# A two-block transformer kernel: column-group sums for the convolution norms, and the norms' learned scale and shift on another engine

## The chip, the cores and the metric

The kernel runs on one core of one Trainium2 chip. The metric is the device time of one execution in microseconds. One run of the program computes both blocks of the reference for one sequence of 256 tokens, all in 32-bit floats.

## The reference

The first block has two layers on 256 tokens of width 1024. Each layer projects the tokens, runs a gated depthwise convolution of 31 taps over 512 channels with a layer norm and a SiLU behind it, runs a neighbourhood attention of 8 heads, and mixes both. The first layer has a dense feed-forward part, the second a mixture of 8 experts of which each token takes 2. Each layer also adds a gated embedding product. The second block has two layers of window attention and mLSTM, and isn't touched here.

```
def first_block(...):
    h = layer_norm(x, ln_in_g, ln_in_b)
    for i in range(DEPTH):
        ...
        conv_out = conformer_conv(a, g, conv_w[i], conv_b[i], conv_ln_g[i], conv_ln_b[i])
        attn_out = neighbourhood_attention(qkv[:, :, 0], qkv[:, :, 1], qkv[:, :, 2], rpb[i])
        mix = jnp.concatenate([conv_out, attn_out], axis=-1) @ w_out[i] + b_out[i]
        h = layer_norm(DEEPNORM_ALPHA * h + mix, ln1_g[i], ln1_b[i])
        j = i // 2
        if i % 2 == 0:
            f = swiglu(h, ffn_w1[j], ffn_w3[j], ffn_w2[j])
        else:
            f = moe_swiglu(h, w_router[j], moe_w1[j], moe_w3[j], moe_w2[j])
        e = jax.nn.sigmoid(h @ ple_gate_w[i] + ple_gate_b[i]) * (p[i] @ ple_w[i])
        h = layer_norm(DEEPNORM_ALPHA * h + f + e, ln2_g[i], ln2_b[i])
    return h
```

## The kernel before, in words

Features lie on the 128 partitions and tokens along the free axis, so the 1024 features are 8 chunks of 128x256 (`KC` = 8) and the 512 convolution channels are 4 (`CC` = 4). The program is written out by hand, one instruction stream for each engine: TensorE (PE), VectorE (DVE), ScalarE (ACT) and the queue of SyncE (SP), which issues all loads. The streams meet at semaphores. The order of the work is the order in which it is written; no scheduler moves it. `fill` names a PSUM bank and waits until the bank's last reader is done; `tile` is the reader's wait for that bank.

**Weights** come as units of 1 MB. SP loads them ahead in a ring of 6 slots, and of 13 in the expert stage (`ring_places`). `load` waits until PE has used the slot's last unit. The addresses of the expert units depend on the routing, so SP waits for `order_out` (L2348, the cast that ends `by_tokens`) before it issues the first of them, and from there on SP runs as far ahead as the slots let it.

[...] `norm_mean` multiplies every chunk by a 128x128 matrix of ones, one full matrix product for each chunk. Where a norm is in `FOLDED_MEAN` or `FOLDED_VAR`, the sum is made otherwise: `group_sum` gives each of four chunks its own group of 32 columns (`COL`), the four products lie side by side, ACT copies the parts to SBUF (`parts_copy`, L1651), and one more product of 128x256 adds them up (`fold_parts`). The norms `conv0` and `conv1` are made in the plain way before. For them PE makes the mean after the first of two value units in `block1_projection` (L592), and the variance at its end. ACT makes the inverse root (L1630), DVE scales (L2155), ACT applies the SiLU with the learned scale and shift (`conv_silu`, L1719), and in `half_pair` PE waits for all four chunks (`conv_mixed`). Ahead of that, `condition_turns` waits for `cond_row`, an ACT copy (L1663) that stands behind `conv_silu` in ACT's stream.

**The learned scale and shift** of the norms `in`, `ln1_0`, `ln2_0`, `ln1_1` and `ln2_1` are DVE instructions (`layer_gain`, L2172) that alternate with the scaling of the next chunk (L2155). Each raises `norm_out`, for which the matrix products of the next stage wait chunk by chunk.

**The routing** of layer 1 follows `ln1_1`. In `router_beside_embedding` PE computes the logits, a 128x8 product for each chunk and each 128 tokens, with one of the last four products of the embedding behind each of the first four chunks. It then transposes the tokens (`turn_tokens`, L800) and waits in `places` for `chosen_out`. DVE ranks the experts of each token in `routing`: five dependent instructions for each half of the tokens, then the choice (L2311), then a copy and four instructions for the gate weights (L2313 to L2318). `by_tokens` takes the counts from PSUM (L2334) and ends in `order_out`. PE goes on with a gate unit, `gather`, and the expert groups.

## Time and profile before

| | |
|---|---|
| Median of 3 runs | 1993.35 us (1993.34 to 1994.25) |
| The profiled execution | 1994.45 us |
| Its span in the trace | 1992.4 us |
| PE busy | 1965.0 us, 99% |
| DVE busy | 753.0 us, 38% |
| ACT busy | 404.5 us, 20% |
| Weights and inputs read | 507.40 MB, 255 GB/s over the span |

Times in the trace count from the span's start; the span is about 2 us shorter than the execution's own time, since what lies ahead of the first instruction and behind the last isn't in it. The stages are, roughly: first norm to 15.6 us, layer 0 to 399, of which the dense feed-forward part is 157 to 386, layer 1 up to the routing to 531, routing and gathering to 564, the experts to 1410, and the second block to the end. A 32-bit product appears in the trace as two records. The engine name PEld is TensorE's weight load.

### The profile page before, as it was taken

Reading aid. Unit: us, or ns where it says so; the run is one execution under the profiler, and the core shown is the slowest. Engines: PE = TensorE matmul, PEld = TensorE weight load, DVE = VectorE, ACT = ScalarE, POOL = GpSimd, SP = SyncE. Lnnn points to the kernel's source line nnn. Section 1 sums busy time; section 2 is a strip of 40 time slices with the busy share of each in tenths; the row PEclk is TensorE's granted clock in tenths of the full one; section 3 lists DMA queues with packets and bytes.
Section 4 is the critical chain, followed back from the end, with each engine's and each line's share of the span. In section 5 each row is a group of like instructions: output and inputs, shape, how many; then the busy total and the mean of one; then the engine's idle time right before and its main releaser. Section 6 shows DMA issues by size and latency. Waiting matters only on the chain.

```text
span 1992.4 us, 36529 instructions
## 1 busy us (share of the span) xinstructions
PE 1965.0 (99%) x15708; PEld 1422.1 (71%) x15708; DVE 753.0 (38%) x1766; ACT 404.5 (20%) x953; POOL 0.2 (0%) x4
## 2 busy tenths in 40 slices
PE   9999999999999999999999999999999999999998
PEld 8879999888766656666666666556664578566797
DVE  6847555586511111111111111111317734426725
ACT  1242110104310111000100010000214442223343
POOL 0000000000000000000000000000000000000000
PEclk9999999999999999999999999999999999999999
DMA  9473644544299999999999999999321211122220
GB/s 353 171 296 146 210 169 176 189 171 190 78 420 420 421 420 421 420 420 420 415 420 420 420 421 419 420 420 420 138 106 55 95 48 59 64 106 85 106 85 22
DMA packets 74929, 510.86 MB, mean 256 GB/s; under 512 B 7888, under 2 KB 13200, under 8 KB 13968
## 3 DMA queue, kind: packets, MB, share of 16 engines
q1 hardware_dynamic: 74768, 508.51, 63.7%
q8 instruction: 126, 2.06, 0.4%
q14 instruction: 35, 0.29, 0.0%
HBM read 507.40 MB, written 1.08 MB: 255 GB/s over the span
## 4 chain that ended last, share of the span: by engine, by line
PE 93%; DMA 4%; DVE 2%; ACT 1%; issue 0%; SPq 0%; DVEq 0%; ACTq 0%
PE ps L483 91%; DMA ring<-weights 4%; PE ps L1313 1%; PE ps L852 1%; PE ps L713 0%; DVE work L2155 0%; SPq L1581 0%; DVE xc L2172 0%; DVE spare L2776 0%; DVE work L2167 0%; PE ps L1473 0%; DVE small L2951 0%; ACT work L1964 0%; ACT work L1630 0%; DVE work L2948 0%
## 5 line engine op out<-in xcount | busy, mean ns | idle before, releaser
L483 PE MATMUL ps<-work 128*32 128x256 f32 (+8 forms) x4912 | 515.6, 375 | 3.2 <-DVE work L2471 0.9
L483 PE MATMUL ps<-work,ring 128*128 128x256 f32 (+2 forms) x1992 | 503.9, 407 | 1.0 <-DVE work L2916 1.0
L483 PEld LDWEIGHTS ps<-work 128*32 128x32 f32 (+3 forms) x4912 | 344.9, 142 | 134.0 <-issue 68.4
L483 PEld LDWEIGHTS ps<-work,ring 128*128 128x128 f32 x1992 | 338.9, 190 | 138.0 <-issue 110.6
L483 PE MATMUL ps<-ring,work 128*32 128x256 f32 (+3 forms) x4392 | 405.8, 407 | 2.7 <-DMA ring<-weights 2.1
L483 PEld LDWEIGHTS ps<-ring,work 128*32 128x32 f32 (+1 forms) x4392 | 234.3, 120 | 129.2 <-issue 59.3
L483 PE MATMUL ps<-xc,ring 128*128 128x256 f32 (+1 forms) x1344 | 254.9, 350 | 1.9 <-DVE xc L2172 1.9
L483 PEld LDWEIGHTS ps<-xc,ring 128*128 128x128 f32 x1344 | 223.5, 191 | 34.4 <-issue 7.3
L2429 DVE TENSOR_TENSOR work<-work,ps 128x256 f32<-128x256 f32 x42 | 17.7, 422 | 411.2 <-ACT work L1797 411.2
L1797 ACT ACTIVATE work<-ps 128x256 f32<-128x256 f32 x42 | 16.2, 385 | 556.1 <-PE ps L483 556.1
L483 PE MATMUL ps<-spare,work 128*32 128x256 f32 (+1 forms) x1128 | 120.4, 427 | 2.5 <-DMA ring<-weights 1.3
L483 PE MATMUL ps<-xc,work 128*128 128x256 f32 (+1 forms) x624 | 117.2, 346 | 0.0
L483 PEld LDWEIGHTS ps<-xc,work 128*128 128x128 f32 x624 | 102.7, 191 | 16.3 <-issue 4.2
L2204 DVE SCALAR_TENSOR_TENSOR work<-work,par 128x256 f32<-128x256 f32 x240 | 98.0, 480 | 0.9
L2392 DVE TENSOR_TENSOR work<-ps,work 128x512 f32<-128x512 f32 x68 | 47.1, 692 | 92.7 <-PE ps L483 92.4
L483 PEld LDWEIGHTS ps<-spare,work 128*32 128x32 f32 x1128 | 52.2, 110 | 38.3 <-issue 21.6
L2550 DVE TENSOR_TENSOR work<-ring 128x512 f32<-128x512 f32 x52 | 33.6, 688 | 51.1 <-PE ps L483 51.1
L483 PE MATMUL ps<-work,con 128*32 128x256 f32 (+1 forms) x262 | 45.3, 390 | 5.8 <-DVEq L2501 1.5
L2443 DVE TENSOR_TENSOR work<-work 128x512 f32<-128x512 f32 x14 | 9.7, 693 | 97.6 <-ACT work L1803 97.6
L483 PE MATMUL ps<-xc,spare 128*128 128x256 f32 x192 | 44.3, 392 | 0.0
L483 PEld LDWEIGHTS ps<-xc,spare 128*128 128x128 f32 x192 | 37.3, 196 | 7.8 <-issue 1.7
L483 PEld LDWEIGHTS ps<-work,con 128*32 128x32 f32 (+1 forms) x262 | 27.8, 151 | 19.0 <-issue 7.9
(284 smaller groups left out, 1254.8 us busy)
## 6 DMA issues: line engine op xcount, KB each, us to landing
ring<-weights SPq DMA_DIRECT2D x287, 1024.0 KB, 13.6
work<-weights SPq DMA_DIRECT2D x130, 1024.0 KB, 19.2
spare<-weights SPq DMA_DIRECT2D x54, 1024.0 KB, 18.9
work<-rel SPq DMA_DIRECT2D x8, 512.0 KB, 12.7
spare<-rows SPq DMA_DIRECT2D x2, 2048.0 KB, 9.2
con<-consts SPq DMA_DIRECT2D x1, 1368.0 KB, 22.1
work<-x_t SPq DMA_DIRECT2D x1, 1024.0 KB, 4.9
xc<-ctx_t SPq DMA_DIRECT2D x1, 1024.0 KB, 27.2
```

Of the source, the lines that this page charges most:

```text
L483: ins = eng.matmul(o, lhs, rhs, start=start, stop=stop, **kw)
L852: last = eng.transpose(o[:, k * P:k * P + P], pair_a[:, n % 2, k * P:k * P + P], ident)
L1313: last = eng.transpose(o[:, kt * P:kt * P + P], prob2_flat[:, at:at + P], ident)
L1797: eng.activation(pair_s[:, n % 2, :], o[:, 0:GW], ACT.Silu).then_inc(s["pair_silu"], 1)
L2204: ins = eng.scalar_tensor_tensor(out=conv_acc[:, j, :], in0=src, scalar=w, in1=conv_acc[:, j, :], op0=ALU.mult, op1=ALU.add)
L2392: return eng.tensor_tensor(r, o.rearrange("p (a b) -> p a b", b=T), r, ALU.add)
L2429: eng.tensor_tensor(pair_a[:, n % 2, :], pair_s[:, n % 2, :], o[:, GW:2 * GW], ALU.mult)\
L2443: eng.tensor_tensor(v, v, rows(gate_row, 2), ALU.mult).then_inc(s["first_weighted"], 1)
L2550: ins = eng.tensor_tensor(up_sum(i, z), in0, in1, op)
```

## The change

Four things are changed. The norms `conv0` and `conv1` are summed on column groups, with the fold of the mean in the middle of the second value unit and the fold of the variance behind the first condition rows of `block1_attention`. The learned scale and shift of `in`, `ln1_0`, `ln2_0` and `ln1_1` become ACT instructions (`gain`); DVE then only scales. The last four embedding products stand behind all logits. On DVE the routing comparisons of both token halves are one instruction each, and the gate weights are made after `by_tokens`. `mean_parts`, `var_parts` and `fold_parts` get a bank and a number of chunks, and `token_sums` waits for `norm_out`, which another engine raises now.

```diff
@@ -78,8 +78,8 @@
-FOLDED_MEAN = ["in", "ln2_0", "ln2_1"]
-FOLDED_VAR = ["ln1_0", "ln2_0", "ln1_1", "ln2_1", "rms0"]
+FOLDED_MEAN = ["in", "conv0", "ln2_0", "conv1", "ln2_1"]
+FOLDED_VAR = ["conv0", "ln1_0", "ln2_0", "conv1", "ln1_1", "ln2_1", "rms0"]
@@ -504,34 +504,35 @@
-            def group_sum(o, c, v):
+            def group_sum(o, c, v, chunks=KC):
 
                 q = COL * (c % 4)
-                return mm(o[q:q + COL, 0:T], ones[:, 0:COL], v, c < 4, c >= 4)
+                return mm(o[q:q + COL, 0:T], ones[:, 0:COL], v, c < 4, c >= chunks - 4)
...
@@ -614,10 +615,13 @@
                     w = next_unit()
                     o = fill(("v", l, j), 4 + j, (s["v_out"], 2 * l + j + 1))
                     tokens(w, GW, o[:, 0:T], xc, 0)
+                    if j:
+                        fold_parts("mean", f"conv{l}", 2)
                     tokens(w, GW, o[:, T:2 * T], xc, 1).then_inc(bank_full[4 + j], 1)
                     if j == 0:
-                        norm_mean(f"conv{l}", conv_acc, CC, T, 2)
-                norm_var(f"conv{l}", CC, T, True, 2)
+                        mean_parts(f"conv{l}", conv_acc, 2)
+                for _ in var_parts(f"conv{l}", True, 3):
+                    pass
@@ -662,6 +666,7 @@
             def block1_attention(l):
                 eng.wait_ge(s["cond_ready"], 1)
                 condition_rows(l, 0)
+                fold_parts("var", f"conv{l}", 2)
@@ -775,21 +780,20 @@
                     if c == KC - 1:
                         last.then_inc(bank_full[0], 1)
-                    if c < 4:
-                        next(products)
-                assert next(products, "ended") == "ended"
+                for _ in products:
+                    pass
...
-                o = fill(("counts",), 1, (s["order_out"], 1))
+                o = fill(("counts",), 6, (s["order_out"], 1))
...
-                o = fill(("places",), 0, (s["places_out"], 1))
+                o = fill(("places",), 4, (s["places_out"], 1))
@@ -1633,6 +1637,13 @@
+            def gain(name, g, b, first=0, end=KC):
+
+                for c in range(first, end):
+                    eng.wait_ge(s["norm_scaled"], before(name) + c + 1)
+                    eng.activation(xc[:, c, 0:T], cen[:, c, :], ACT.Identity, bias=par[:, PC(b, c)],
+                                   scale=par[:, PC(g, c)]).then_inc(s["norm_out"], 1)
+
@@ -2082,6 +2093,7 @@
             eng.wait_ge(s["params_loaded"], 16)
+            gain("in", "ln_in_g", "ln_in_b")
@@ -2092,7 +2104,10 @@
                 norm(f"ln1_{l}", KC, T)
-                ple_products(l)
+                gain(f"ln1_{l}", f"ln1_g{l}", f"ln1_b{l}", 0, 4)
+                ple_products(l, 0, 1)
+                gain(f"ln1_{l}", f"ln1_g{l}", f"ln1_b{l}", 4)
+                ple_products(l, 1)
@@ -2101,7 +2116,9 @@
                     norm("ln2_0", KC, T)
+                    gain("ln2_0", "ln2_g0", "ln2_b0", 0, 2)
                     condition_rows(1, -1)
+                    gain("ln2_0", "ln2_g0", "ln2_b0", 2)
@@ -2294,23 +2311,24 @@
+                eng.tensor_copy(by_expert[:, 4], con[:, CN.all("bases")])
...
-                for t in range(TT):
-                    other = logits[:, t, :].unsqueeze(1).broadcast_to([P, 8, 8])
...
-                    link(eng.tensor_tensor(gc, other, own, ALU.is_gt))
-                    link(eng.tensor_tensor(ge, other, own, ALU.is_equal))
-                    link(eng.tensor_tensor(ge, ge, before, ALU.mult))
-                    link(eng.tensor_tensor(gc, gc, ge, ALU.add))
-                    link(eng.tensor_reduce(rank_t[:, t, :], gc, AX.X, ALU.add))
+                other = logits.unsqueeze(2).broadcast_to([P, TT, 8, 8])
+                own = logits.unsqueeze(3).broadcast_to([P, TT, 8, 8])
...
+                eng.tensor_tensor(gc, other, own, ALU.is_gt)
+                link(eng.tensor_tensor(ge, other, own, ALU.is_equal))
+                link(eng.tensor_tensor(ge, ge, before.unsqueeze(1).broadcast_to([P, TT, 8, 8]), ALU.mult))
+                link(eng.tensor_tensor(gc, gc, ge, ALU.add))
+                link(eng.tensor_reduce(rank_t, gc, AX.X, ALU.add))
                 eng.tensor_scalar(rank_t, rank_t, float(TOP_K), None, ALU.is_lt).then_inc(s["chosen_out"], 1)
                 eng.wait_ge(s["chosen_out"], 1)
-                link(eng.tensor_copy(by_expert[:, 4], con[:, CN.all("bases")]))
+
+            def gate_weights():
+
                 eng.wait_ge(s["gate_exp"], 2)
@@ -3029,10 +3049,11 @@
-                norm(f"ln1_{l}", res, KC, T, layer_gain(f"ln1_g{l}", f"ln1_b{l}", xc))
+                norm(f"ln1_{l}", res, KC, T, None)
                 if l == 1:
                     routing()
                     by_tokens()
+                    gate_weights()
                     places()
@@ -3040,7 +3061,7 @@
-                norm(f"ln2_{l}", res, KC, T, layer_gain(f"ln2_g{l}", f"ln2_b{l}", xc))
+                norm(f"ln2_{l}", res, KC, T, layer_gain("ln2_g1", "ln2_b1", xc) if l else None)
```

PE's stream at the end of `block1_projection` and the start of `block1_attention`, before (`work,con` is a sum with the matrix of ones, `ring,work` with 32 rows the condition rows, 128x2x2 the condition turns, the last row the first `half_pair`):

```order
L483 MATMUL ps<-ring,xc 128x256 x16
L483 MATMUL ps<-work,con 128x256 x4
L483 MATMUL ps<-ring,xc 128x256 x16
L483 MATMUL ps<-work,con 128x256 x4
L483 MATMUL ps<-ring,work 32x256 x16
L483 MATMUL ps<-work 128x256 x4
L483 MATMUL ps<-ring,work 32x256 x16
L483 MATMUL ps<-con,work 128x2x2 x2
L483 MATMUL ps<-work,ring 128x256 x8
```

and with the change:

```order
L483 MATMUL ps<-ring,xc 128x256 x16
L483 MATMUL ps<-work,con 32x256 x4
L483 MATMUL ps<-ring,xc 128x256 x8
L483 MATMUL ps<-work,con 128x256
L483 MATMUL ps<-ring,xc 128x256 x8
L483 MATMUL ps<-work,con 32x256 x4
L483 MATMUL ps<-ring,work 32x256 x16
L483 MATMUL ps<-work,con 128x256
L483 MATMUL ps<-work 128x256 x4
L483 MATMUL ps<-ring,work 32x256 x16
L483 MATMUL ps<-con,work 128x2x2 x2
L483 MATMUL ps<-work,ring 128x256 x8
```

Each sum of four full products became four on column groups and one fold; the fold of the variance is 16 condition-row products later than the sum was.

PE's stream at the routing, before against after (`par,xc` are the logits, `work,ring` the embedding products, `con,xc` the transposes):

```order
-L483 MATMUL ps<-par,xc 128x8 x2
-L483 MATMUL ps<-work,ring 128x256
-L483 MATMUL ps<-par,xc 128x8 x2
-L483 MATMUL ps<-work,ring 128x256
-L483 MATMUL ps<-par,xc 128x8 x2
-L483 MATMUL ps<-work,ring 128x256
-L483 MATMUL ps<-par,xc 128x8 x2
-L483 MATMUL ps<-work,ring 128x256
-L483 MATMUL ps<-par,xc 128x8 x8
-L800 MATMUL ps<-con,xc 128x128 x16
+L483 MATMUL ps<-par,xc 128x8 x16
+L483 MATMUL ps<-work,ring 128x256 x4
+L804 MATMUL ps<-con,xc 128x128 x16
```

The 16 logit products now stand in one piece, and the four embedding products between them and the transposes.

ACT's stream at norm `ln2_0` with the change (L1634 is the inverse root, L1644 the gain, L1674 the copy of the condition row for which PE waits):

```order
L1634 ACTIVATE work<-ps,con 128x256
L1644 ACTIVATE xc<-work,par 128x256 x2
L1674 ACTIVATE work<-ps 128x256
L1644 ACTIVATE xc<-work,par 128x256 x6
L1719 ACT_TABLE_LOAD
```

Before, the copy stood directly behind the inverse root; now two gains are ahead of it.

## Rows read from the trace of the kernel before

**Rows 1.** Windows, experts: stretch, length, busy PE/PEld/DVE/ACT/POOL, clock, DMA share, GB/s
```profile
564.00:1410.00 846.00, 840.31 (x8986) 535.02 (x8987) 104.31 (x186) 74.09 (x162) 0.00 (x0) 1.00 1.01 419
```

**Rows 2.** Chain of waits, late in the expert stage: start us, us, what
```profile
1319.04 26.87 DMA ring<-weights
1346.04 3.66 PE ps L483 x64
```

**Rows 3.** Waits of the whole span, PE on weights: total us, times, longest
```profile
PE ps L483 <- DMA ring<-weights: 3.4, 4, 1.3
```

**Rows 4.** Timeline, PE and DVE, first norm: start us, us, engine, line [idle before]
```profile
15.64 14.70 PE L483 MATMUL ps<-xc,ring 128*128 128x256 f32 x61 [0.57 <-DVE xc L2172]
...
15.09 0.41 DVE L2172 TENSOR_SCALAR xc<-work,par 128x256 f32<-128x256 f32 x1
...
19.04 0.73 DVE L2172 TENSOR_SCALAR xc<-work,par 128x256 f32<-128x256 f32 x2
```

**Rows 5.** Groups of ACT by shape, modulate: busy us, mean ns
```profile
L1700 ACT ACTIVATE work<-work,small 128x256 f32<-128x256 f32 x16 | 8.1, 588 | 2.4 <-DVE work L2683 2.4
```

**Rows 6.** Timeline, PE, start of the dense feed-forward stage
```profile
154.61 2.02 PE L483 MATMUL ps<-xc,ring 128*128 128x128 f32 x16 [0.73 <-DVE xc L2172]
156.91 2.02 PE L483 MATMUL ps<-xc,ring 128*128 128x128 f32 x16 [0.28 <-DVE xc L2172]
```

**Rows 7.** Timeline, PE and ACT, norm ln2_0
```profile
397.45 0.61 PE L483 MATMUL ps<-con,work 128*128 128x4 f32 x4 [0.84 <-ACT work L1663]
398.39 6.89 PE L483 MATMUL ps<-xc,ring 128*128 128x256 f32 x22 [0.33 <-DVE xc L2172]
...
397.03 0.38 ACT L1663 ACTIVATE work<-ps 128x256 f32<-128x256 f32 x1
```

**Rows 8.** Timeline, PE, a sum on column groups and what follows it
```profile
527.60 0.64 PE L483 MATMUL ps<-work,con 128*32 128x256 f32 x8
528.17 1.13 PE L483 MATMUL ps<-work,ring 128*128 128x256 f32 x4
```

**Rows 9.** Timeline, PE, around the variance sum of conv0
```profile
80.90 7.07 PE L483 MATMUL ps<-ring,xc 128*128 128x256 f32 x32
87.81 1.89 PE L483 MATMUL ps<-work,con 128*128 128x256 f32 x8
89.63 1.93 PE L483 MATMUL ps<-ring,work 128*32 128x256 f32 x32
...
94.42 0.61 PE L483 MATMUL ps<-con,work 128*128 128x4 f32 x4
94.89 3.70 PE L483 MATMUL ps<-work,ring 128*128 128x256 f32 x16
```

**Rows 10.** Timeline, ACT, around the same sum
```profile
89.74 0.47 ACT L1630 ACTIVATE work<-ps,con 128x256 f32<-128x256 f32 x1 [6.76 <-PE ps L483]
...
93.51 0.36 ACT L1663 ACTIVATE work<-ps 128x256 f32<-128x256 f32 x1
```

**Rows 11.** Timeline, PE, logits and routing
```profile
535.10 1.85 PE L483 MATMUL ps<-par,xc 128*128 128x8 f32 x16
537.21 1.97 PE L800 MATMUL ps<-con,xc 128*128 128x128 f32 x16 [0.27 <-DVE small L2294]
540.39 1.25 PE L483 MATMUL ps<-small,con 128*128 128x8 f32 x10 [1.21 <-DVE small L2311]
541.50 8.84 PE L483 MATMUL ps<-xc,spare 128*128 128x256 f32 x32
```

**Rows 12.** Timeline, DVE, routing after the choice
```profile
541.31 0.17 DVE L2334 COPY work<-ps 128x8 f32<-128x8 f32 x1
...
543.45 0.17 DVE L2348 CAST crowded<-work 128x8 int32<-128x8 f32 x1
```

**Rows 13.** Windows around both falls of the clock, columns as in Rows 1
```profile
399.00:403.00 4.00, 4.00 (x12) 2.95 (x12) 3.75 (x14) 0.00 (x0) 0.00 (x0) 0.57 0.69 244
542.00:547.00 5.00, 5.00 (x17) 4.09 (x16) 4.62 (x19) 0.00 (x0) 0.00 (x0) 0.66 0.22 66
```

More of the change, by code:

```diff
@@ L505, in norm_mean @@
                 last.then_inc(bank_full[bank], 1)
-            def group_sum(o, c, v):
+            def group_sum(o, c, v, chunks=KC):
                 q = COL * (c % 4)
-                return mm(o[q:q + COL, 0:T], ones[:, 0:COL], v, c < 4, c >= 4)
-            def mean_parts(name, src):
-                o = fill(("mean_parts", name), 0, (s["norm_sums"], SUMS["mean", name]))
-                for c in range(KC):
+                return mm(o[q:q + COL, 0:T], ones[:, 0:COL], v, c < 4, c >= chunks - 4)
@@ L515, in mean_parts @@
+            def mean_parts(name, src, bank=0):
+                o = fill(("mean_parts", name), bank, (s["norm_sums"], SUMS["mean", name]))
+                for c in range(chunks_of(name)):
                     if normk(name) > 1:
                         eng.wait_ge(*source(name, c))
-                    last = group_sum(o, c, src[:, c, 0:T])
-                last.then_inc(bank_full[0], 1)
-            def var_parts(name, centred):
-                o = fill(("var_parts", name), 1, (s["norm_sums"], SUMS["var", name]))
-                for c in range(KC):
+                    last = group_sum(o, c, src[:, c, 0:T], chunks_of(name))
+                last.then_inc(bank_full[bank], 1)
@@ L524, in var_parts @@
+            def var_parts(name, centred, bank=1):
+                chunks = chunks_of(name)
+                o = fill(("var_parts", name), bank, (s["norm_sums"], SUMS["var", name]))
+                for c in range(chunks):
                     eng.wait_ge(s["norm_squared"], before(name) + c + 1)
-                    last = group_sum(o, c, squares(name, centred)[:, c, 0:T])
-                    if c == 3:
+                    last = group_sum(o, c, squares(name, centred)[:, c, 0:T], chunks)
+                    if c == chunks - 1:
+                        last.then_inc(bank_full[bank], 1)
+                    if c % 4 == 3:
@@ L527, in var_parts, with fold_parts @@
                         yield
-                last.then_inc(bank_full[1], 1)
-                yield
-            def fold_parts(kind, name):
-                b, read_by = (1, (s["norm_sums"], SUMS["std", name])) if kind == "var" else \
-                    (0, (s["norm_centered"], before(name) + KC))
+            def fold_parts(kind, name, bank=0):
+                b, read_by = (bank + 1, (s["norm_sums"], SUMS["std", name])) if kind == "var" else \
+                    (bank, (s["norm_centered"], before(name) + chunks_of(name)))
@@ L1750, in block1_attention, with ple_products @@
                             .then_inc(s["nbr_turned"], 1)
-            def ple_products(l):
-                for c in range(4):
+            def ple_products(l, first=0, end=KC // 2):
+                for c in range(first, end):
                     o = tile(eng, "ple", l, c)
@@ L3023, in _ @@
             eng.wait_ge(s["x_loaded"], 16)
-            norm("in", res, KC, T, layer_gain("ln_in_g", "ln_in_b", xc), beside=prepare)
+            norm("in", res, KC, T, None, beside=prepare)
             for l in range(DEPTH):
```

10 lines of the change are left out of this document (5 added, 5 removed).

## The prediction

> **What bounds the kernel now.** The first page shows PE busy for 99% of the span, so only PE's own work, its few waits and its clock can be worth anything; DVE and ACT idle most of the time. I then cut the span by stage. The expert stage holds 846 of the 1992 us, and in it two things are full at once: PE is busy for 840.31 us and the 16 DMA engines have a share of 1.01 at 419 GB/s [rows 1]. The chain of waits says which of the two ends last: late in the stage it runs through a weight transfer of 26.87 us, which PE waits for at 1346.04 us [rows 2]. PE waits only 3.4 us for weights in all, in four places [rows 3]. So the transfers, running without a pause from the first expert unit on, set the end of the stage, and PE is some 3.4 us ahead of them. That stage ends earlier by as much as its first load is issued earlier, which is the moment of `order_out`, and what PE alone gains behind the routing is lost in a longer wait for weights. Everything ahead of `order_out` counts in full if it lies on PE's path. Behind the experts nothing is changed.
>
> **First norm.** The first product of the projection starts at 15.64 us, just behind the first gain, and the eight gains of DVE run from 15.09 us to 19.04 + 0.73 = 19.77 us [rows 4], slower than the 0.43 us in which PE eats a chunk (two records of 7.07/32 = 0.22 us each, [rows 9]). On ACT the trace has the same kind of instruction, an activation with scale and shift from SBUF: 588 ns long, 8.1/16 = 0.51 us apart [rows 5]. It starts when DVE has scaled the first chunk, about 14.87 us, so the first chunk comes at 15.46 us where DVE's came at 15.50, and the last at 15.46 + 7 x 0.51 = 19.0 us. **Gain 0.8 us.**
>
> **`ln1_0`.** PE waits for chunk 3 until 154.61 us and for chunk 7 until 156.91 us [rows 6]. From the same first scaling (151.82 us) ACT delivers chunk 3 at 154.0 us, then makes one copy of embedding products (0.5 us), and delivers chunk 7 at 156.5 us. With 0.14 us from gain to PE the second wait ends at 156.6 us. **Gain 0.3 us.** DVE's token sums start earlier and bind nothing.
>
> **`ln2_0`.** Here the order on ACT costs something. PE's last condition turns wait for the row copy, which ends at 397.41 us [rows 7]. With the change two gains stand ahead of it, and the first can't start before 397.62 us, so the copy ends at 397.62 + 2 x 0.51 + 0.38 = 399.0 us and the projection starts at about 399.5 us where it started at 398.39 [rows 7]. The gains then come faster than before. The clock matters too: between 399 and 403 us the granted clock averages 0.57, that is, mostly 1.2 GHz, after PE had waited 0.84 and 0.33 us and had done small products between [rows 7, 13]. PE does its first products at half clock either way and enters that stretch later. I take **a loss of 0.8 us**; the bounds are 1.1 us lost (the whole delay) and 0.2 us gained (at full clock the last chunk ends the first product, and it comes 0.2 us earlier).
>
> **The convolution norms.** A sum of four full products takes 89.63 - 87.81 = 1.82 us [rows 9]; four on column groups take 528.17 - 527.60 = 0.57 us [rows 8], and the fold is one product more, 0.43 us. That is 0.8 us of PE for each of two sums in each of two layers, 3.3 us in all. But the fold of the variance comes behind the condition rows, and everything on ACT comes behind the fold. Before, ACT started the inverse root at 89.74 us and was done with root, table load, four SiLUs and the row copy at 93.51 + 0.36 = 93.87 us [rows 10], 4.13 us later, and PE wanted the row at 94.42 us [rows 9]: slack 0.55 us. Now relative to the start of the variance sum: rows start at +0.57, the fold at +2.4, the root at +3.1 (before: +1.93), so the row is copied at +7.2, while PE arrives at 6.61 - 1.82 + 0.57 + 0.43 = +5.8. PE waits 1.4 us and resumes 0.6 to 0.7 us later than before, against the 0.7 to 0.8 us that the mean's sum, which has no such wait behind it, saved. On the way the scores wait for the root too, since their bank is the one that it reads, but that wait is inside the same 1.4 us. **Net nothing in each layer**; the bounds are 1.5 us gained, where the chain is shorter than its rows, and 0.5 us lost.
>
> **Logits and routing.** Before, PE paced the logits: the last four chunks end at 535.10 + 1.85 = 536.95 us [rows 11]. Now the first chunk is there at 531.33 us, a chunk follows every 0.51 us (one copy between), and the last at 535.3 us, so the logits end at about 535.9 us, 1.05 us earlier. The embedding products (4 x 0.43 us) and the transposes (1.97 us, [rows 11]) follow without a wait, and PE reaches the counts at 539.4 us where it was at 540.39. It had waited 1.21 us there for DVE's choice [rows 11]; now DVE has five dependent instructions fewer (10 of 0.26 us became 5 of about 0.3) and is done at about 538.2 us, so PE comes last, and DVE's saving is worth only what it takes out of that wait. DVE took the counts at 541.31 us [rows 12], 0.4 us after they were there, because the gate weights came first; now it takes them at 539.95. The 2.3 us up to the cast [rows 12] are unchanged. At full clock `order_out` comes **1.35 us earlier**. The gate weights are paid behind it, where PE is busy with a gate unit of 8.84 us [rows 11] and hides them.
>
> **The clock in this place.** After the waits of 0.27 and 1.21 us, with 128x8 products around the second, the clock fell: 0.66 on average from 542 to 547 us [rows 13], and 32 records took 8.84 us [rows 11] that take 7.07 at 2.4 GHz [rows 9], a price of 1.77 us, free before, since the expert stage waits for weights anyway. In the dense stage idle times of 0.73 and 0.28 us with wide products between them did no such thing (the first there stayed 2.02 us long, [rows 6]). So narrow products seem to count almost as idle time, and the change puts all 16 of them in one piece of over 4 us. I expect the clock to fall during or behind it, in front of `order_out`, where the slower products and transposes are on the path. If it falls on those wholly the price is 1.77 us, if early part of it hides in the pace of ACT; I take 1.2 us, bounds 0 and 2.5. The Trainium skill (TensorE: Matmul & The Clock Gate, HAM oscillation) says that only long idle gaps of TensorE throttle it again; the trace disagrees, with falls after waits of 1.21 us at most. By the rule the clock would stay up here, which is the first rival.
>
> **The sum**, against the profiled execution's 1994.45 us: -0.8 - 0.3 + 0.8 + 0 - 1.35 + 1.2 = -0.45 us, so 1994.0. The median, 1993.35 us, is 1.1 us below that execution; I apply the difference to it: **1992.9 us**. No difference is to be measured: 0.2%, 4 us, is about what a measurement of this kernel can tell from no change.
>
> **Rivals.**
> A, the clock holds through the logits: 0.45 + 1.2 us off the median, so **1991.7 us**. For it: PE has almost no idle time there, only narrow products. Against it: the contrast above.
> B, the new wait in the convolution norms becomes the dearer side, and the kernel is **slower**. Two idle stretches of about 0.7 us each, with narrow turns beside them, are like those ahead of the fall at 399 us [rows 13]. If the clock falls behind them, the next products take 1.77 us more in that layer: 1992.9 + 1.8 = 1994.7 us with one layer, 1996.4 with both. It decides when PE's waits between fold and turns pass roughly the 1.2 us of [rows 7]. Against it: between the two stand 32 wide records of condition rows.
> C, the fold's chain is short and PE hardly waits: the two waits of 1.4 us fall away, about **1990.1 us**. It needs ACT to finish 1.4 us sooner than its rows say.
> D, the transfers don't bind the expert stage, and PE's start there counts: it gains 1.0 us for the counts and 1.77 us for a gate unit at full clock in place of the net 0.15 us, about **1990.3 us**. The saturated DMA and the chain speak against it [rows 1, 2].
>
> **How the numbers follow.** The forecast 0.52, A 0.2, B 0.13, C 0.06, D 0.04, the rest for something unseen. Between them they span 1990.1 to 1996.4 us. The range 1990.2 to 1995.4 leaves out C's lower side, B with both layers, and most of the unseen. None of the named cases passes 4 us: faster by over 0.2% 0.06 (C with A), slower by over 0.2% 0.04 (B in both layers with the worst bounds), 0.90 in between.
>
> **What would show it.** The first projection's opening wait unchanged, but its first unit about 0.8 us shorter; PE idle twice before the turns of each attention stage, the turns waiting for the row copy by over 0.5 us; turns of `ln2_0` 1.5 us later against the copy of the variance; a granted clock of 0.50 somewhere between 533 and 541 us and none on the gate unit; the cast of the routing within 0.5 us of its old place; PE's waits for weights in the expert stage growing from 3.4 us to 5 or more. It would be wrong if `order_out` moved by 1 us or more, if conv waits were absent, or if the expert stage got shorter than from `order_out` to its end before.

## The result, and the profile after

| | before | after |
|---|---|---|
| Median of 19 runs each | 1993.36 us (1992.27 to 1994.59) | 1998.12 us (1996.68 to 2000.16) |
| The profiled execution, its span | 1994.45, 1992.4 us | 1999.24, 1997.5 us |
| Cast of the routing (`order_out`) starts | 543.45 us | 548.18 us |
| From the cast to the last instructions of the chain | 1443.9 us | 1444.3 us |

The ratio of after to before is 1.0024, interval 1.0018 to 1.0030. The kernel is **slower by 4.8 us**, and the prediction was wrong: 1992.9 us, with a range up to 1995.4 us.

The last two lines of the table say where to look. The chain of waits of the changed kernel has these late pieces (start us, us, what), the first two of the same kind as those in [rows 2]:

```profile
1323.32 28.04 DMA ring<-weights
1351.50 3.66 PE ps L483 x64
...
1992.45 2.38 DVE work L2184 x6
```

The last wait for weights ends at 1351.50 us, where it ended at 1346.04 us: 5.5 us later. The last DVE instructions start at 1992.45 us; in the chain of before they start at 1987.34 us. From the start of the cast to the end of that weight wait it is 803.3 us, before 802.6 us. So the expert stage only shifted with the cast, as the prediction says of it, and all of the loss is made ahead of 548.18 us. The window of the expert stage answers to [rows 1] (stretch, length, busy PE, PEld, DVE, ACT, POOL, clock, DMA share, GB/s), and the waits of PE for weights to [rows 3] (total us, times, longest):

```profile
564.00:1410.00 846.00, 837.82 (x8965) 534.67 (x8967) 105.96 (x188) 73.68 (x163) 0.00 (x0) 1.00 1.01 420
```

```profile
PE ps L483 <- DMA ring<-weights: 4.4, 3, 2.2
```

PE waits 1.0 us more for the ring. Behind the routing it had gained 1.7 us (its first gate unit takes 7.15 us now, not the 8.84 of [rows 11]), and the stretch from the cast to the end is none the shorter. That the gain turned into just these waits isn't shown: x4_three below has the same 7.15 us and waits 3.6 us in all.

**First norm and `ln1_0`.** PE's timeline (start us, us, engine, line, operation, output<-input, tile, count, and in brackets the idle time before and what ended it), to be held against [rows 4, 6]:

```profile
14.90 2.36 PE L483 MATMUL ps<-xc,ring 128*128 128x256 f32 x9 [0.61 <-ACT xc L1644]
...
156.22 2.02 PE L483 MATMUL ps<-xc,ring 128*128 128x128 f32 x16 [0.42 <-ACT xc L1644]
```

The start at 14.90 us isn't the change's: the variance sum of the first norm already begins at 9.24 us where it began at 10.01. Over all traces of this case that start lies anywhere from 8.95 to 10.12 us, so I count every place below from it. From there to the mean sum of `conv0` (79.18 us before, 77.59 after) it is 69.17 us before and 68.35 us after: the gains on ACT are worth **0.82 us**.

**The convolution norm.** PE, DVE and ACT around both sums of `conv0`, columns as above. These rows answer to [rows 9, 10]:

```profile
77.59 0.64 PE L483 MATMUL ps<-work,con 128*32 128x256 f32 x8
...
81.71 0.59 PE L483 MATMUL ps<-work,con 128*128 128x256 f32 x2
...
85.69 0.64 PE L483 MATMUL ps<-work,con 128*32 128x256 f32 x8
87.26 1.93 PE L483 MATMUL ps<-ring,work 128*32 128x256 f32 x32 [0.93 <-issue]
89.13 0.70 PE L483 MATMUL ps<-work,con 128*128 128x256 f32 x2
90.48 1.13 PE L483 MATMUL ps<-work 64*128 64x256 f32 x8 [0.66 <-ACT work L1634]
91.55 1.93 PE L483 MATMUL ps<-ring,work 128*32 128x256 f32 x32
94.14 0.58 PE L483 MATMUL ps<-con,work 128*128 128x4 f32 x4 [0.66 <-ACT work L1674]
...
84.28 2.28 DVE L2250 TENSOR_TENSOR work<-work,con 128x2048 f32<-128x2048 f32 x1
86.48 0.68 DVE L2258 TENSOR_TENSOR work<-ps,par 128x512 f32<-128x512 f32 x1
...
89.86 0.47 ACT L1634 ACTIVATE work<-ps,con 128x256 f32<-128x256 f32 x1 [3.08 <-PE ps L483]
...
93.63 0.36 ACT L1674 ACTIVATE work<-ps 128x256 f32<-128x256 f32 x1
```

PE is idle three times: 0.93 us ahead of the first condition rows, 0.66 us for the inverse root (L1634) and 0.66 us for the copied row (L1674). The last two I had foreseen, as 1.4 us; the rows show 1.32. The first I had not. The condition rows go to bank 5, and the last reader of bank 5 is DVE's bias add to the second value unit (L2258), which ends at 86.48 + 0.68 = 87.16 us, behind the mask of 2.28 us. The profile gives this wait only as "issue"; that it is the bank, x5_bank shows below. Before, the full variance sum of 1.82 us [rows 9] stood in front of the same rows and covered this read. DVE in the trace of before:

```profile
83.04 2.28 DVE L2233 TENSOR_TENSOR work<-work,con 128x2048 f32<-128x2048 f32 x1
...
88.01 0.69 DVE L2241 TENSOR_TENSOR work<-ps,par 128x512 f32<-128x512 f32 x1 [2.69 <-PE ps L483]
```

There the mask was done at 85.32 us, DVE sat idle until PE had filled the bank, and the bias add began 0.20 us behind the start of the variance sum (87.81 us). In the changed kernel it begins 0.79 us behind it (85.69 us), because the mean comes later: it is folded in the middle of the second value unit, and DVE's subtraction of it and the mask come behind the fold. So by the rows about 0.6 of the 0.93 us comes from the mean's late fold, and only the rest from the shortened variance sum alone. This split is an estimate; no run folds the variance alone.

From the mean sum to the turns it is 94.14 - 77.59 = 16.55 us, before 94.42 - 79.18 = 15.24: **1.31 us lost**. Layer 1 shows the same three waits.

**`ln2_0`.** PE and ACT, answering to [rows 7]:

```profile
398.35 1.02 PE L483 MATMUL ps<-con,work 128*128 128x4 f32 x4 [2.42 <-ACT work L1674]
399.23 21.14 PE L483 MATMUL ps<-xc,ring 128*128 128x256 f32 x85
...
396.94 1.09 ACT L1644 ACTIVATE xc<-work,par 128x256 f32<-128x256 f32 x2 [0.49 <-DVE work L2172]
397.94 0.36 ACT L1674 ACTIVATE work<-ps 128x256 f32<-128x256 f32 x1
```

PE waits 2.42 us in one piece where it waited 0.84 us. Behind the start of this wait its clock is low, and for longer than before, which the windows below show.

**Logits and routing.** PE and DVE, answering to [rows 11, 12]:

```profile
534.33 2.00 PE L483 MATMUL ps<-par,xc 128*128 128x8 f32 x16 [0.46 <-ACT xc L1644]
536.69 2.94 PE L483 MATMUL ps<-par,xc 128*128 128x8 f32 x16 [0.36 <-ACT xc L1644]
539.48 3.76 PE L483 MATMUL ps<-work,ring 128*128 128x256 f32 x8
543.03 2.56 PE L804 MATMUL ps<-con,xc 128*128 128x128 f32 x16
...
546.46 7.15 PE L483 MATMUL ps<-xc,spare 128*128 128x256 f32 x32
...
541.74 0.17 DVE L2327 TENSOR_SCALAR small<-small 128x16 f32<-128x16 f32 x1
546.04 0.17 DVE L2352 COPY work<-ps 128x8 f32<-128x8 f32 x1 [4.13 <-PE ps L483]
...
548.18 0.17 DVE L2366 CAST crowded<-work 128x8 int32<-128x8 f32 x1
```

DVE has its choice at 541.9 us and then waits 4.13 us for PE. PE is late because it works at half clock. Eight records of embedding products take 3.76 us; at 2.4 GHz eight such records take 1.97 us (below, in the kernel with fillers). From the first logit to the cast it is 13.85 us, before 543.45 - 531.51 = 11.94 us. The windows around both falls of the clock, columns as in [rows 1]:

```profile
397.00:401.00 4.00, 2.65 (x8) 2.37 (x9) 2.56 (x10) 4.00 (x9) 0.00 (x0) 0.57 0.29 123
401.00:405.00 4.00, 4.00 (x12) 3.19 (x11) 0.00 (x0) 1.52 (x2) 0.00 (x0) 0.57 0.83 315
537.00:541.00 4.00, 4.00 (x19) 3.73 (x19) 1.24 (x7) 2.07 (x5) 0.00 (x0) 0.57 0.00 0
541.00:545.00 4.00, 4.00 (x19) 3.44 (x18) 0.81 (x4) 1.71 (x2) 0.00 (x0) 0.58 0.00 0
```

A mean of 0.57 over 4 us is 3.4 us at 1.2 GHz and the rest at 2.4. Each fall lasts 6.8 us here; each of those in [rows 13] lasted 3.4 us.

**The account up to the cast**, in us, counted from the variance sum of the first norm, after less before: first norm -0.82, `conv0` +1.31, `ln1_0` -0.41, `conv1` +1.31, `ln2_0` +2.2, routing 13.85 - 11.94 = +1.91. The sum is +5.5. The cast moved by 4.73, since this execution began its variance sum 0.77 us earlier. The figure for `ln2_0` is the stretch from its first condition turns to the first logit (141.23 us before, 144.74 after) without the 1.31 us of `conv1`. Between the medians there are 4.8 us, 0.7 us less than this account; it rests on one trace of each kernel, and the difference stays open.

### The profile page after: what moved, and what is told of

Same layout as the page of the kernel before. It is cut to its first block, busy times and chain, and to the rows that moved or that the text cites. A ratio compares the mean times of both kernels' runs of the same rounds, so it can differ in the third digit from the quotient of the medians.

```text
span 1997.5 us, 36545 instructions
## 1 busy us (share of the span) xinstructions
PE 1964.0 (98%) x15716; PEld 1420.8 (71%) x15716; DVE 741.5 (37%) x1729; ACT 421.4 (21%) x989; POOL 0.2 (0%) x4
## 3 DMA queue, kind: packets, MB, share of 16 engines
HBM read 507.40 MB, written 1.08 MB: 255 GB/s over the span
## 4 chain that ended last, share of the span: by engine, by line
PE 92%; DMA 4%; ACT 1%; DVE 1%; issue 1%; SPq 0%; DVEq 0%; ACTq 0%
PE ps L483 90%; DMA ring<-weights 3%; DMA work<-weights 1%; PE ps L1317 1%; PE ps L856 1%; ACT xc L1644 0%; PE ps L718 0%; ACT work L1730 0%; SPq L1585 0%; DVE spare L2796 0%; ACT work L1634 0%; DVE work L2184 0%; PE ps L1477 0%; ACT L1730 0%; DVE small L2971 0%
## 5 line engine op out<-in xcount | busy, mean ns | idle before, releaser
L1808 ACT ACTIVATE work<-ps 128x256 f32<-128x256 f32 x42 | 16.1, 383 | 558.3 <-PE ps L483 558.3
L1852 ACT ACTIVATE work<-ps 128x256 f32<-128x256 f32 x52 | 19.9, 383 | 101.0 <-PE ps L483 101.0
```

Of the source, the lines that this page charges most:

```text
L1808: eng.activation(pair_s[:, n % 2, :], o[:, 0:GW], ACT.Silu).then_inc(s["pair_silu"], 1)
L1852: eng.activation(snap[n % 2][:, at:at + T], o[:, 0:T], ACT.Copy).then_inc(s["snap_out"], 1)
```

## Experiments

Every kernel was run beside the kernel before in the same job; its ratio is to that. "Cast, counted" is the start of the cast less the start of the first norm's variance sum in the profiled execution: 533.44 us before, 538.94 us after. The kernels x1 to x4 ran in one job, x5, x6, y2 and y3 in a second, z1, z2, y1 and b2 in a third; the median of the kernel before was 1993.60, 1993.76 and 1993.27 us in them, and 1993.36 us beside the changed kernel. So a difference between medians of two jobs is uncertain by up to 0.5 us.

| kernel | median us (runs) | ratio, interval | low clock ahead of the cast, us | cast, counted | first logit to cast |
|---|---|---|---|---|---|
| x1_logits | 1995.72 (11) | 1.0011, 1.0002 to 1.0020 | 3.4 at 399; 3.4 at 539 | 535.62 | 11.82 |
| x2_conv | 1993.94 (11) | 1.0003, 0.9994 to 1.0012 | 6.8 at 397; 3.4 at 537 | 535.01 | 12.29 |
| x3_ln2 | 1995.84 (11) | 1.0011, 1.0002 to 1.0020 | 3.4 at 397; 6.8 at 534 | 536.31 | 13.72 |
| x4_three | 1989.48 (11) | 0.9982, 0.9973 to 0.9991 | 3.4 at 396 | 530.63 | 10.70 |
| x5_bank | 1994.75 (11) | 1.0005, 0.9996 to 1.0014 | 3.4 at 397; 6.8 at 534 | 535.44 | 13.90 |
| x6_meanonly | 1987.85 (6) | 0.9974, 0.9962 to 0.9986 | none | 528.24 | 10.70 |
| y2_behind | 1992.50 (11) | 0.9993, 0.9984 to 1.0002 | 6.8 at 530 | 532.40 | 13.80 |
| y3_filler | 1989.96 (11) | 0.9983, 0.9974 to 0.9992 | none | 530.22 | 11.61 |
| z1_only_ln2 | 1992.03 (11) | 0.9995, 0.9986 to 1.0004 | 3.4 at 399 | 531.79 | 10.71 |
| z2_only_conv | 1992.32 (11) | 0.9999, 0.9990 to 1.0008 | 3.4 at 536 | 533.29 | 11.93 |
| y1_only_logits | 1996.93 (11) | 1.0017, 1.0008 to 1.0027 | 3.4 at 398; 6.8 at 535 | 536.76 | 15.31 |
| b2_spins | 1989.90 (11) | 0.9985, 0.9976 to 0.9994 | none | 528.26 | 10.71 |

### First: undo one place at a time, then all three

x1_logits puts the embedding products back between the logits of the changed kernel:

```diff
+                    if c < 4:
+                        next(products)
-                for _ in products:
-                    pass
+                assert next(products, "ended") == "ended"
```

> The changed kernel with the last four embedding products back between the logits, all else as changed. Theory (the piece of 16 narrow products makes the clock fall ahead of the cast that releases the expert weights): the clock stays at 2.4 GHz through logits, products and transposes, the cast moves about 2 to 3 us earlier relative to the first logit product (from 14.0 us to about 11 to 12), and the time falls by 2 to 3 us from 1998.1 to about 1995.5. Rival (the gains on ScalarE set the pace and the delay, not the clock): at most 0.5 us back, 1997.6.

Measured: 1995.72 us, 2.4 us below the changed kernel. The clock still fell once, for 3.4 us, on the transposes, and the first logit to the cast took 11.82 us.

x2_conv makes the norms `conv0` and `conv1` in full sums again:

```diff
-FOLDED_MEAN = ["in", "conv0", "ln2_0", "conv1", "ln2_1"]
+FOLDED_MEAN = ["in", "ln2_0", "ln2_1"]
-                    if j:
-                        fold_parts("mean", f"conv{l}", 2)
...
-                        mean_parts(f"conv{l}", conv_acc, 2)
+                        norm_mean(f"conv{l}", conv_acc, CC, T, 2)
-                for _ in var_parts(f"conv{l}", True, 3):
-                    pass
+                norm_var(f"conv{l}", CC, T, True, 2)
...
-                fold_parts("var", f"conv{l}", 2)
```

> The changed kernel with the convolution norms summed as before, in full products. Theory (the fold behind the condition rows lengthens ScalarE's chain, and the condition rows wait for the value bias in their bank): PE waits nowhere between variance sum and half_pair, 1.1 us back in each layer, about 2.2 us in all, so about 1996.0. Rival (the folded sums save PE time elsewhere and their waits are covered): the time goes up by 1.4 to 3 us, to 1999.5 or more.

Measured: 1993.94 us, 4.2 us below the changed kernel, the most of the three, and 2.1 us below the time that I expected. Mean sum to turns is 92.95 - 77.71 = 15.24 us again, as before. Of the 4.2 us the two layers account for 2.6 directly; the fall of the clock at the routing was also 3.4 us shorter in the trace.

x3_ln2 copies the row ahead of all eight gains of `ln2_0`:

```diff
-                    gain("ln2_0", "ln2_g0", "ln2_b0", 0, 2)
                     condition_rows(1, -1)
-                    gain("ln2_0", "ln2_g0", "ln2_b0", 2)
+                    gain("ln2_0", "ln2_g0", "ln2_b0")
```

> The changed kernel with ScalarE's copy of the condition row ahead of all eight gains of norm ln2_0. Theory (the two gains ahead of the copy hold PE 1.6 us longer, and this idle time makes the clock fall a second time): the wait before the turns goes from 2.42 us to about 0.8, the half-speed time behind it from about 7 us to 3.4 or none, 2 to 2.5 us back, about 1995.8. Rival (only the order on ScalarE counts, the clock falls as long as before): 1.1 us back, about 1997.0.

Measured: 1995.84 us, 2.3 us below the changed kernel. The wait for the row is 0.84 us again and the fall behind it 3.4 us, not 6.8.

x4_three makes all three of these edits. It keeps the first norm, `ln1_0`, the gains of `ln2_0` on ACT, and the choice in one go.

> All three of these together: what is left of the change is the scale and shift on ScalarE and the routing comparisons in one go. Theory (the three parts are the whole loss, and what is left is a gain in the first norm, in ln1_0 and in routing): below the kernel before, about 1990.5 to 1991.5. Rival (ScalarE's gains are themselves a loss): 1994 or more.

Measured: 1989.48 us, ratio 0.9982, **faster than the kernel before**, and 8.6 us below the changed kernel. The three undone singly give 2.4 + 4.2 + 2.3 = 8.9 us. So what is left of the change is worth about 4 us, and three places spoil it. The cast, counted, explains 533.44 - 530.63 = 2.8 us of the 4; the rest isn't accounted for. PE's timeline of this kernel at the routing:

```profile
534.71 1.97 PE L801 MATMUL ps<-con,xc 128*128 128x128 f32 x16 [0.27 <-DVE small L2307]
536.88 1.25 PE L483 MATMUL ps<-small,con 128*128 128x8 f32 x10 [0.20 <-DVE small L2323]
```

The wait for the choice is 0.20 us where it was 1.21 us [rows 11], and the first logit to the cast takes 10.70 us, not 11.94: DVE's shorter choice and its later gate weights together gain 1.24 us, and the fall of the clock that followed this wait in [rows 13] is gone too.

### Second: how each place loses

x5_bank is the changed kernel with the first condition rows in bank 6, which is free:

```diff
-                    bank = 1 if n else 5
+                    bank = 1 if n else 6
```

> The changed kernel with the first condition rows of each layer in bank 6 instead of bank 5, whose last reader is the value bias add on VectorE. Theory (PE's 0.93 us of idle time before the condition rows is that reader): the 0.93 us go, the fold, the root, the SiLUs and the row copy come 0.9 us earlier, and each layer is 0.9 us shorter from variance sum to half_pair (8.9 to about 8.0 us); 1.5 to 2 us in all, about 1996.3. Rival (another wait ends at the same time, or ScalarE's chain starts late for another reason): less than 0.3 us per layer.

PE's timeline at `conv0`:

```profile
85.82 0.64 PE L483 MATMUL ps<-work,con 128*32 128x256 f32 x8
86.27 1.91 PE L483 MATMUL ps<-ring,work 128*32 128x256 f32 x32
...
89.47 1.13 PE L483 MATMUL ps<-work 64*128 64x256 f32 x8 [0.66 <-ACT work L1634]
...
93.13 0.58 PE L483 MATMUL ps<-con,work 128*128 128x4 f32 x4 [0.66 <-ACT work L1674]
```

Measured: the wait of 0.93 us is gone, the two of 0.66 us stay. Variance sum to the first half (the attention's first wide products) takes 93.56 - 85.82 = 7.74 us; it took 8.89 in the changed kernel and 7.08 before. The bank is therefore shown as the cause of 1.15 us in each layer, and the root and the row still cost 0.66 us more than the full sum did. From the mean sum to the turns it is 93.13 - 77.71 = 15.42 us here, against 15.24 before: with this wait gone, both folds together lose 0.2 us, near the nothing that I had forecast. In the median this kernel is 3.4 us faster than the changed one, 1.1 us more than two layers explain; its trace has the shorter fall at `ln2_0`.

x6_meanonly is x4_three with the mean of the convolution norms on column groups and the variance in a full sum:

```diff
+FOLDED_MEAN = ["in", "conv0", "ln2_0", "conv1", "ln2_1"]
 FOLDED_VAR = ["ln1_0", "ln2_0", "ln1_1", "ln2_1", "rms0"]
...
+                    if j:
+                        fold_parts("mean", f"conv{l}", 2)
...
+                        mean_parts(f"conv{l}", conv_acc, 2)
...
                 norm_var(f"conv{l}", CC, T, True, 2)
```

> As the run with three parts undone, but with the mean of the convolution norms still on column groups; only their variance is summed in full. Theory (the mean's fold costs nothing, since nobody waits for it early; only the variance's fold is on the path): 0.7 us less per layer, about 1988.1. Rival (the late mean fold delays VectorE's mask and value bias, and the condition rows wait for their bank or the scores for the values): 1989.5 or more.

```profile
85.31 1.89 PE L483 MATMUL ps<-work,con 128*128 128x256 f32 x8
87.13 1.93 PE L483 MATMUL ps<-ring,work 128*32 128x256 f32 x32
88.99 1.14 PE L483 MATMUL ps<-work 64*128 64x256 f32 x8
90.06 1.93 PE L483 MATMUL ps<-ring,work 128*32 128x256 f32 x32
91.92 0.61 PE L483 MATMUL ps<-con,work 128*128 128x4 f32 x4
```

Measured: 1987.85 us, ratio 0.9974, the fastest kernel here: 5.9 us below the kernel before in the same job. PE has no wait at all in this place, and mean sum to turns takes 91.92 - 77.30 = 14.62 us, 0.62 less than before. The saving of the mean is real (I had 0.7 to 0.8 us). Its late fold delays DVE here too, but the full variance sum covers that. With the mean folded, folding the variance as well costs 16.55 - 14.62 = 1.93 us. The trace also has no fall of the clock ahead of the cast, and the granted clock over the whole run is 0.999 in five of the six runs, as in the traced one. Twice 0.62 us is 1.24 of the 1.6 us between the medians of this kernel and x4_three.

y2_behind is x4_three with the embedding products behind the logits, as in the change. y3_filler is the same with a useless product of ones behind each of the first four pairs of logits; its output is read by nobody:

```diff
                         last.then_inc(bank_full[0], 1)
+                    if c < 4:
+                        mm(ps[:, 7, 0:T], ones, res[:, 0, :], True, True)
                 for _ in products:
```

> The run with three parts undone, but with the last four embedding products behind all logits again: this part alone. Theory (narrow products in one piece make the clock fall): at least one stretch of 3.4 us at 1.2 GHz between the first logit and the cast, the cast 1 to 2.5 us later than in the run with three parts undone (10.7 us after the first logit), about 1991.0 to 1992. Rival (the order is neutral or good by itself): within 0.5 us of 1989.5.

> As the run with the products behind the logits, plus one useless full-width product of 128x256 behind each of the first four logit chunks, in the place where the embedding products stood. It adds 1.7 us of work to PE. Theory (the clock follows how much of the time is filled with wide products): the clock stays at 2.4 GHz up to the cast, and the cast comes no later than without the filler although there is more work: about 1991. Rival (the clock falls for another reason, such as the short waits for ScalarE's gains): it falls all the same, and the filler costs its 1.7 us, about 1993.

PE in y2_behind, and then in y3_filler:

```profile
527.71 2.00 PE L483 MATMUL ps<-par,xc 128*128 128x8 f32 x16 [0.45 <-ACT xc L1640]
530.07 3.28 PE L483 MATMUL ps<-par,xc 128*128 128x8 f32 x16 [0.36 <-ACT xc L1640]
533.20 3.76 PE L483 MATMUL ps<-work,ring 128*128 128x256 f32 x8
```

```profile
531.49 0.68 PE L483 MATMUL ps<-work,con 128*128 128x256 f32 x2
532.00 1.85 PE L483 MATMUL ps<-par,xc 128*128 128x8 f32 x16
533.70 1.97 PE L483 MATMUL ps<-work,ring 128*128 128x256 f32 x8
```

Their windows over the same 4 us:

```profile
530.00:534.00 4.00, 3.94 (x18) 3.85 (x19) 0.55 (x5) 2.45 (x6) 0.00 (x0) 0.55 0.00 0
```

```profile
530.00:534.00 4.00, 4.00 (x31) 3.82 (x31) 0.12 (x1) 3.15 (x7) 0.00 (x0) 1.00 0.00 0
```

Measured: the order alone costs 3.0 us (1992.50 against 1989.48 us), and with four more products of 0.43 us the kernel is 2.5 us **faster** than without them. The embedding products take 3.76 us in the one and 1.97 us in the other. The granted clock over the whole run is 0.999 in nine of the eleven runs of y3_filler, and in one of the eleven of y2_behind. That the loss at the logits is the clock, and that wide products among the logits keep it up, is shown. The filler also fills PE's wait of 0.36 us between the logits; y1_only_logits below has the fall without any wait of that size. My expectation for y2_behind was too low on both counts: the cast comes 13.80 - 10.70 = 3.1 us later, where I had at most 2.5, and the median lies 0.5 us above my range.

The Trainium skill (TensorE: Matmul & The Clock Gate, HAM oscillation) ties throttling to long idle gaps. Between 527.71 and 533.20 us of y2_behind the trace lists one idle gap of PE, 0.36 us, and the clock falls in that stretch; the rule doesn't cover this case.

### Third: each place alone, and a remedy

z1_only_ln2 is x4_three with the order on ACT of the change in `ln2_0`; z2_only_conv is x4_three with the convolution norms of the change; y1_only_logits is the kernel before with one edit, the products behind the logits.

> Keeps of the change only the first norm, ln1_0 and the order on ACT in ln2_0 (two gains ahead of the row copy); reference point is the kernel with all three places undone, 1989.5 us. Theory (the order makes PE idle 2.4 us in one piece where it had idled 0.84, and the clock then stays low for 6.8 us in place of 3.4): cast 2.0 to 2.6 us later than 539.7, so about 1991.8 us. Rival (my prediction's term, at most 1.1 us by the delay of the copy): 1990.3 us or less.

Measured: 1992.03 us, as the theory has it, 2.5 us above x4_three. But its trace shows the long wait (2.42 us) and then a fall of only 3.4 us, and the cast, counted, 531.79 - 530.63 = 1.16 us later. So the order itself costs 1.2 us when the fall is no longer than otherwise, and 2.6 us in the changed kernel's trace against x3_ln2's (538.94 - 536.31), where it is twice as long. Over all the traces, each of one run: five have this long wait (the changed kernel, x1_logits, x2_conv, x5_bank, z1_only_ln2), and the fall there lasts 6.8 us in two and 3.4 us in three; the nine others have a fall of 3.4 us there in four and none in five. The runs of z1_only_ln2 differ as well: six have a granted clock of 0.998, like the traced one, and a mean of 1991.6 us; the other five have 0.997 or 0.996 and a mean of 1992.9 us. What decides between the two lengths stays open.

> Keeps of the change the first norm, ln1_0 and both convolution norms on column groups, with the logits and ln2_0 as before; reference 1989.5 us. Theory (1.3 us lost by PE in each layer through bank 5, root and row): 2.6 us later, 1992.1 us, if the clock is left alone. Rival (the two stages also bring a fall of the clock somewhere ahead of the cast, which the kernel with them undone does not have, and each fall costs up to 1.7 us more): 1993.5 us or more, with a low stretch that the reference lacks.

Measured: 1992.32 us, 2.8 us above x4_three. Mean sum to turns is 94.11 - 77.55 = 16.56 us, that is 1.32 us lost in each layer, 2.6 us in all. The low stretch of x4_three at 396 us is absent, and one at 536 us is there in its place, on the transposes (3.59 us for 16). So the rival's condition is met in part and its time isn't: the falls nearly cancel.

> The kernel before, with the embedding products behind the logits as its only change. Theory (16 narrow products in one piece bring the clock down ahead of the transposes and it stays low for 6.8 us): the first logit to the cast takes 13.8 us as in the other two kernels with this order, cast 1.5 to 3 us later than 543.45, 1995 to 1996.5 us. Rival A (the order itself is worth the 1.35 us that I predicted and the fall comes only together with the other parts): 1992 us, no low stretch ahead of 542 us. Rival B (the fall at 542 us that the kernel before has anyway is only moved): within 0.5 us of 1993.4.

```profile
531.20 5.65 PE L483 MATMUL ps<-par,xc 128*128 128x8 f32 x32 [0.48 <-DVE xc L2171]
536.70 3.76 PE L483 MATMUL ps<-work,ring 128*128 128x256 f32 x8
...
543.65 1.28 PE L483 MATMUL ps<-small,con 128*128 128x8 f32 x10 [0.62 <-ACT work L1771]
```

Measured: 1996.93 us, 3.7 us above the kernel before. A single moved statement makes the kernel slower by nearly 0.2%, 0.4 us more than the top of my range. The first logit to the cast takes 15.31 us, not 13.8 as I wrote: here the choice is still made half by half, and PE reaches the counts with a wait of 0.62 us. Both rivals fall. All 32 logit records form one row here, in which PE has no idle time long enough to be listed, and the clock is at its lower level from before the row's end: the mean over 535 to 539 us is 0.52.

The three places added one at a time to x4_three cost 2.5 (z1), 2.8 (z2) and 3.0 us (y2), 8.3 in all; together 8.6. They hardly interact.

b2_spins is x6_meanonly with useless 128x128 products of ones where PE idles in `ln2_0`:

```diff
+                spin(2)
                 fold_parts("var", "ln2_0")
+                spin(5)
                 condition_turns(1, -1, mod_t).then_inc(bank_full[5], 1)
+                spin(2)
```

> The best kernel so far (mean on column groups, variance in full sums, 1987.9 us) with two, five and two useless 128x128 products of ones around the variance fold and the condition turns of ln2_0, where PE idles. Theory (idle time between narrow products is what brings the clock down at 397 to 403 us): no low stretch there in any run, projection's first product not above 2.1 us, 1986.8 to 1987.6 us. Rival (the idle time is hidden behind nothing and the useless products delay the turns): 1988 us or more, by up to nine records of 0.055 us, 0.5 us.

Measured: 1989.90 us, 2.0 us above x6_meanonly, which ran in another job. The theory's time fell. Up to the cast the two traces are the same to 0.02 us (528.26 and 528.24), so the useless products neither cost nor gain. (Their 18 records start about 0.11 us apart in PE's idle time; my rival counted nine of 0.055 us.) In x6_meanonly there was no fall left for them to prevent. The profiled execution loses its time later, in parts where both kernels are alike: a wait for weights of 2.09 us, behind it 3.4 us of low clock in the expert stage (mean 0.66 over 1336 to 1341 us), and 1.08 us of "issue" at 1409.84 us. I have no cause for these, and that the spins cost 2 us in the median is not explained. The clock isn't it: seven of the eleven runs have a granted clock of 0.999, and their mean is 1989.6 us, against 1987.8 us for the five such runs of x6_meanonly.

## Why the prediction was wrong

**What bounds the kernel: right.** The expert stage moved with the cast. From the cast to the last instructions of the chain it is 1442.7 to 1444.5 us in every trace but that of b2_spins (1446.1), though the cast itself lies anywhere from 537.19 to 548.18 us; PE's faster gate unit, 1.7 us, didn't shorten the stretch in the changed kernel (1444.3 us, before 1443.9). Rival D falls with it. The waits for weights grew to 4.4 us, where the prediction asked for 5 or more.

**First norm, `ln1_0`: right in mechanism and size.** 0.8 us forecast, 0.82 measured; 0.3 forecast, 0.38 (x4_three) to 0.41 (the changed kernel) measured.

**"Net nothing in each layer" is the step that failed in kind.** The prediction followed the variance's chain through root and row, and that part came as written. But it took the condition rows as free to start, "rows start at +0.57". They start in a bank that DVE still reads. The 1.82 us sum that was removed had been hiding that reader, and the mean's late fold holds the reader up further; so PE waits 0.93 us. 1.31 us lost per layer, against bounds of 0.5 us lost and 1.5 gained. Rival B came out on the right side by the wrong mechanism: it needed a fall of the clock behind the turns, and no trace shows one there.

**`ln2_0`, "a loss of 0.8 us": mis-sized.** About 2.2 us in the trace of the changed kernel, 1.2 us where the fall stays as short as it was (z1_only_ln2). The delay of the row copy was seen, and its bound of 1.1 us is nearly what z1_only_ln2 shows; what was missed is that a longer wait ahead of the narrow turns can come with a fall of 6.8 us in place of 3.4, as two of the five traces with that wait show.

**Logits and routing: "-1.35" was right, "clock +1.2" was mis-sized, and so the sign of the pair was wrong.** The fall came where it was forecast, on the narrow products, so rival A falls. It lasted 6.8 us, not 3.4. y3_filler, at full clock, takes 11.61 us from the first logit to the cast with four needless products in it. Without them the last logits would wait for ACT's last gain: it starts at 531.60 us there, the first at 527.67, and the first logit follows the first gain by 0.74 us. So the last logit record would start at about 532.7 us and not at 533.59, and the stretch would be about 10.7 us, an estimate. By it the full-clock gain of the change is 1.2 us, where I had 1.35, and all of it is the 1.24 us that x4_three shows with the old order of the products: the new order gains nothing even at full clock. The price of the clock is 13.85 - 10.7 = 3.15 us, where I took 1.2 with a bound of 2.5; 13.80 against 10.70 us in y2_behind and x4_three gives 3.1. The bound came from a single fall of [rows 13] on one gate unit and left no room for a fall twice as long. Net +1.9 us, not -0.15.

The three errors, 2.6 + 1.4 + 2.1 us, make the 6 us between the forecast -0.45 and the +5.5 of the trace's account. The prediction named its own sign of failure, a cast that moves by 1 us or more, and it moved by 4.73 us.

## What to carry to other kernels

Before you remove or shorten a matrix product, look at what its time covers besides itself: here a sum of 1.8 us hid DVE's read of the bank that comes next, and with the sum shortened to 0.6 us, and DVE later by 0.6 us through the mean's fold, PE stood waiting for that read. Put work later in a chain only where the wait behind it is covered: the mean's fold alone gained 0.62 us per layer, and the variance's fold on top of it lost 1.93. Keep wide products between narrow ones on TensorE; gathering the narrow ones for tidiness cost 3 us here, and useless wide products between them bought 2.5 us back.

## What the hardware showed that I had not expected

- TensorE's clock fell here while it was busy with 128x8 products. In y2_behind the only listed idle time among 5.5 us of logits is 0.36 us, and the granted clock is 0.55 over the next 4 us; with four 128x256 products among the same logits it is 1.00.
- A fall lasts 3.4 us or 6.8 us in these traces ahead of the cast, nothing between. Five of the six kernels with all logits in one piece have the 6.8 us there, one (x2_conv) 3.4.
- Waits of like size end differently. A wait for weights of 2.2 us in the changed kernel brings no fall, one of 2.09 us in b2_spins is followed by 3.4 us at 1.2 GHz.
- The first norm's variance sum begins anywhere from 8.95 to 10.12 us over the 14 traces, a spread of 1.2 us that has to be taken off before traces are compared at this scale. With one trace for each kernel it isn't shown whether it belongs to the kernel or to the run.
